# Hybrid encoder block on one core: the first expert tile's input from early rows and 0/1 products, tile tables by matmuls

## The reference, cut to what matters

```python
logits = (hf @ w_router + b_router)
top_vals, top_idx = lax.top_k(logits, 4)
gates = softmax(top_vals)
flat_e = top_idx.reshape(-1)
order = argsort(flat_e)                    # pairs sorted by expert
xs = hf[order // 4]
sizes = bincount(flat_e, length=32)
gu = ragged_dot(xs, w_gate_up, sizes) + b_gate_up[e_sorted]
gate, up = minimum(gu[:, :1024], 7), clip(gu[:, 1024:], -7, 7)
act = (up + 1) * (gate * sigmoid(1.702 * gate))
out = (ragged_dot(act, w_down, sizes) + b_down[e_sorted]) * gates_sorted
h = h + segment_sum(out, token_of)
```

## Time and profile before

| what | us |
|---|---|
| median of 3 runs | 2186.11 |
| lowest and highest | 2184.25, 2188.28 |
| profiled execution | 2184.28 |
| its span | 2182.2 |
| granted TensorE clock, mean | 0.982 |

### The profile page before, as it was taken

The page is one execution under the profiler, slowest core; times in us unless marked ns, Lnnn a source line. Parts: engine busy times, 40 slices in busy tenths (PEclk is TensorE's granted clock), DMA queues, the critical chain, the costliest instruction groups (busy, mean ns, idle before and its releaser), DMA issues.

```text
span 2182.2 us, 42210 instructions
## 1 busy us (share of the span) xinstructions
PE 2081.2 (95%) x15590; PEld 1884.4 (86%) x15591; DVE 937.7 (43%) x2300; ACT 433.0 (20%) x1072; POOL 556.5 (26%) x641
## 2 busy tenths in 40 slices
PE   7999999999976889999999999999999999999996
PEld 6777777755546889999999999999999999999996
DVE  1322332233443444554454455444455544454544
ACT  1333333232321111112111111211112111112110
POOL 2211111100223223223323222323222322223332
PEclk9999999999988999999999999999999999999998
DMA  7000000141315889999998998999899998999994
GB/s 254 28 11 11 11 11 1 36 167 49 144 50 184 253 264 324 314 287 295 276 294 280 307 299 278 304 284 312 282 312 302 307 291 262 312 314 306 319 304 113
DMA packets 240403, 477.30 MB, mean 219 GB/s; under 512 B 44607, under 2 KB 60747, under 8 KB 240304
## 3 DMA queue, kind: packets, MB, share of 16 engines
q1 hardware_dynamic: 182416, 433.09, 59.3%
...
...
## 4 chain that ended last, share of the span: by engine, by line
PE 90%; DVE 3%; issue 3%; DMA 1%; ACT 1%; POOL 0%; DVEq 0%; ACTq 0%; SPq 0%; POOLq 0%
PE psum L1011 42%; PE psum L1027 23%; PE psum L811 8%; PE psum L960 5%; PE psum L850 3%; PE psum L919 2%; PE psum L828 2%; PE psum L918 1%; PE psum L892 1%; PE psum L940 1%; PE psum L903 1%; DMA area<-in_w_in 1%; DVE area L1319 1%; DVE area L1314 1%; PE psum L990 1%
## 5 line engine op out<-in xcount | busy, mean ns | idle before, releaser
L1011 PE MATMUL psum<-area 128*128 128x128 f32 (+3 forms) x8192 | 979.0, 282 | 38.2 <-issue 20.1
L1011 PEld LDWEIGHTS psum<-area 128*128 128x128 f32 x8192 | 970.3, 192 | 43.6 <-issue 43.6
L1027 PE MATMUL psum<-area 128*128 128x128 f32 (+3 forms) x4096 | 496.3, 282 | 2.2
L1027 PEld LDWEIGHTS psum<-area 128*128 128x128 f32 x4096 | 484.5, 191 | 11.7 <-DVE area L1319 11.3
L605 POOL DMA_INDIRECT out<-area x160 | 255.9, 1600 | 68.5 <-issue 39.1
L1293 DVE STREAM_TRANSPOSE area<-area 32x320 f32<-32x320 f32 x512 | 257.1, 502 | 15.0
L1300 DVE TENSOR_SCALAR area<-psum,area 128x160 f32<-128x160 f32 x256 | 86.5, 379 | 347.0 <-PE psum L1011 347.0
L1314 DVE TENSOR_SCALAR area<-psum,area 128x160 f32<-128x160 f32 x256 | 86.5, 379 | 266.2 <-PE psum L1011 265.5
L602 POOL COPY area<-area 128x5 uint32 x32 | 6.0, 188 | 714.7 <-ACT area L779 714.7
L811 PE MATMUL psum<-area 128*128 128x128 f32 x1536 | 178.4, 277 | 9.6 <-ACT area L692 4.0
L811 PEld LDWEIGHTS psum<-area 128*128 128x128 f32 x1536 | 175.0, 193 | 14.3 <-ACT area L688 5.8
...
## 6 DMA issues: line engine op xcount, KB each, us to landing
area<-in_w_gate_up SPq DMA_DIRECT2D x256, 1024.0 KB, 6.8
area<-in_w_down SPq DMA_DIRECT2D x128, 1024.0 KB, 5.3
...
area<-in_x SPq DMA_DIRECT2D x9, 512.0 KB, 12.3
...
```

The costliest lines, as they stand in the source:

```text
L1011: ins = mm(dst, w_gu[piece][:, k, c * P:(c + 1) * P], xT[:, PART * s + k, 0:width], start=(s == 0 and k == 0 and c % 2 == 0), stop=(s == 1 ...
L1027: ins = mm(bank[4 + d // 3][:, (d % 3) * SLOTS:(d % 3) * SLOTS + width], w_dn[q][:, kk, d * P:(d + 1) * P], actT[:, 2 * q + kk, 0:width], ...
```

## The change

Tile 0 is now always a tile of expert 0 (a table value makes expert 0 use at least one tile), so that its weights needn't be chosen. Its input `xT` comes from three sources instead of one gather:

- rows of blocks 0 to 5: SyncE reads the list of expert 0 when the scatters of these blocks have landed, GpSimd gathers what it finds (`early_rows`, zeroed before; indices outside are skipped), and VectorE turns the five groups, two behind HB of block 7 and three behind the tables;
- blocks 6 and 7: `by_chunk` holds the normed rows in the order of the 128-wide chunks (block 6 copied by GpSimd, block 7 made by VectorE), `is_place` is a 0/1 matrix of tokens by slots, and 8 matmuls per block form the products in PSUM (steps XTa, XTb, XT); VectorE adds them to `xT`.

The counts come as a column by a matmul, the tiles of each expert by one compare and one sum, and both running sums by one matmul with the constant `upto`. VectorE writes the last normed block and its places only behind all that. In the loop ScalarE issues the next list behind two sigmoids, not ahead of them; GpSimd waits no more for the gathered rows, and VectorE waits for each group apart.

```diff
+    parts["levels"][0, 0] = -1.0
+    parts["floor"] = np.where(p == 0, 1.0, -1.0e6)
+    parts["upto"] = np.concatenate([p <= e[None, :], p < e[None, :]], 1).astype(np.float32)
...
+                    ("HA", e), ("XTa", e - 1), ("HB", e), ("XTb", e - 1), ("RT", e), ("RK", e), ("XT", e)]
 
 
...
-                weights(0, 0, piece, early_in)
+                weights(0, 0, piece, w_exp_in[piece])
             for i in range(NT):
                 b = i % H_ROWS
+                if i == NT - 1:
+                    sp.wait_ge(listed, 16 * (NT - DIRECT) * TOPK)
+                    for q in range(Q):
+                        sp.dma_start(early_list[32 * q:32 * q + 32, :, :],
+                                     lists[0:SLOTS, :].rearrange("(g j) c -> j g c", j=32)).then_inc(early_in, 16)
                 sp.wait_ge(h_ready, 2 * (i + 1))
                 sp.dma_start(out[0][i * P:(i + 1) * P, :], h_sb[b]).then_inc(h_out, 16)
                 sp.wait_ge(hf_ready, i + 1)
-                sp.dma_start(hf_dram[i * P:(i + 1) * P, :], hf).then_inc(hf_out, 16)
+                sp.dma_start(hf_dram[i * P:(i + 1) * P, :], hf if i < NT - 1 else hf_last).then_inc(
+                    hf_out if i < NT - DIRECT else hf_late, 16)
...
-            sp.wait_ge(early_in, 16 * PIECES)
-            with sp.If(e0 < 1):
-                for piece in range(PIECES):
-                    sp.sem_inc(w_exp_in[piece], 16)
-            with sp.Else():
-                for piece in range(PIECES):
-                    weights(e0, 0, piece, w_exp_in[piece])
-            refill(e0, 0, 1)
+            refill(0, 0, 1)
             with sp.Fori(1, MAX_TILES) as t:
                 with sp.If(t < n_tiles):
...
 
             wait(empty_in, 16)
+            wait(pv_done, NT * HEADS)
+            g.tensor_copy(quarter, K["quarter"].to_broadcast([P, G])).then_inc(pick_ready, 1)
+            g.memset(early_rows, 0.0).then_inc(early_picked, 1)
             for n in range(NT):
+                if n == NT - DIRECT:
+                    wait(hf_ready, n + 1)
+                    g.tensor_copy(by_chunk[0].rearrange("t (k p) -> t p k", k=KD), hf.rearrange("t (p k) -> t p k", k=KD)).then_inc(by_chunk_ready, 1)
+                    wait(early_in, 16 * Q)
+                    wait(pick_ready, 1)
+                    g.tensor_tensor(early_pick, early_list[:, :, 0], quarter, ALU.add).then_inc(early_picked, 1)
+                    wait(early_picked, 2)
+                    wait(hf_out, 16 * (NT - DIRECT))
...
+                    sigmoid(t * 2, 0)
+                    sigmoid(t * 2, 1)
                     act.wait_ge(list_read, t + 1)
                     load_list(t + 1)
-                    sigmoid(t * 2, 0)
-                    sigmoid(t * 2, 1)
                     flush_rows(t)
...
                         ins = mm(bank[7][:, 2 * P:2 * P + E], hfT[:, k, :], w_r[:, k, :], start=(k == 0), stop=(k == KD - 1))
                     ins.then_inc(rt_done, 1)
+                if kind in ("XTa", "XTb", "XT"):
+                    j = n - (NT - DIRECT)
+                    pe.wait_ge(placed, j + 1)
+                    pe.wait_ge(by_chunk_ready, j + 1)
+                    for d in {"XTa": range(KD // 2), "XTb": range(KD // 2, KD), "XT": range(KD)}[kind]:
+                        ins = mm(bank[4 + d // 3][:, (d % 3) * SLOTS:(d % 3 + 1) * SLOTS], by_chunk[j][:, d * P:(d + 1) * P],
+                                 is_place[:, j, :], start=(j == 0 and d % 3 == 0), stop=(j == 1), skip_group_check=True)
+                        if j and d in (2, 5, 7):
+                            ins.then_inc(first_done, 1)
+                if kind == "RK" and n == NT - 1:
+                    pe.wait_ge(mask_ready, NT)
+                    mm(bank[3][0:E, 0:1], cums[:, NT, :], ones[:, 0:1], start=True, stop=True).then_inc(count_mm, 1)
                 if kind == "RK":
-                    rank_of(n, bank[4 + n - (NT - 2)][:, 0:E]).then_inc(rank_mm, 1)
-
-            mm(bank[6][:, 0:E], ones, cums[:, NT, :], start=True, stop=True).then_inc(rank_mm, 1)
+                    rank_of(n, bank[4 if n < NT - 1 else 1][:, 0:E]).then_inc(rank_mm, 1)
+                if kind == "RK" and n == NT - 1:
+                    mm(bank[0][:, 2 * E:3 * E], ones, cums[:, NT, :], start=True, stop=True)
+                    pe.wait_ge(used_ready, 1)
+                    mm(bank[0][:, 0:2 * E], used_b[0:E, :], K["upto"][0:E, :], start=True, stop=True).then_inc(total_mm, 1)
+
 
             pe.wait_ge(tab_ready, 1)
             for c, col in enumerate((0, 3, 2)):
...
                     V.tensor_copy(hfT[:, 4:8, :], bank[3].rearrange("p (k n) -> p k n", k=4)).then_inc(hb_read, 1)
+                    if n == NT - 1:
+                        V.scalar_tensor_tensor(by_chunk[1].rearrange("t (k p) -> t p k", k=KD), h_sb[n % H_ROWS].rearrange("t (p k) -> t p k", k=KD),
+                                               rs_h[:, n:n + 1], gf_row.rearrange("t (p k) -> t p k", k=KD),
+                                               ALU.mult, ALU.mult).then_inc(by_chunk_ready, 1)
+                        early_turn(range(2))
...
-                    dve.wait_ge(rank_mm, n - (NT - 2) + 1)
-                    ch.link(V.tensor_tensor(rank_at, bank[4 + n - (NT - 2)][:, 0:E], K["room"], ALU.add))
+                    j = n - (NT - DIRECT)
+                    if j == 0:
+                        dve.wait_ge(lanes_in, 16)
+                    ch.link(V.tensor_scalar(off_list[:, j:j + 1], mask[:, n, 0:1], -OUTSIDE, OUTSIDE, ALU.mult, ALU.add))
+                if kind == "RK" and n == NT - 1:
+                    dve.wait_ge(count_mm, 1)
+                    ch.link(V.tensor_copy(count_c[0:E, :], bank[3][0:E, 0:1]))
+                    ch.link(V.tensor_scalar(over[0:E, :], K["levels"][0:E, :], count_c[0:E, 0:1], None, ALU.is_lt))
+                    ch.link(V.tensor_reduce(used_c[0:E, :], over[0:E, :], AX_X, ALU.add))
+                    V.tensor_copy(used_b[0:E, :], used_c[0:E, 0:1].to_broadcast([E, P])).then_inc(used_ready, 1)
+                if kind == "RK":
+                    dve.wait_ge(rank_mm, j + 1)
+                    ch.link(V.tensor_tensor(rank_at, bank[4 if n < NT - 1 else 1][:, 0:E], K["room"], ALU.add))
+                    V.tensor_scalar(is_place[:, j, :], lane_at, rank_at[:, 0:1], off_list[:, j:j + 1],
+                                    ALU.subtract, ALU.is_equal).then_inc(placed, 1)
+                if kind == "RK" and n < NT - 1:
                     places(n)
 
 
-            dve.wait_ge(rank_mm, 3)
-            dve.wait_ge(hf_out, 16 * NT)
-            dve.wait_ge(h_out, 16 * NT)
-            ch.link(V.tensor_copy(count, bank[6][:, 0:E]))
-            ch.link(V.tensor_scalar(used, count, 0.0, None, ALU.is_gt))
-            for j in range(1, LEVELS):
...
-            total = cum[:, src, :]
-
-
-            tile_no = K["tokp"]
-            ch.link(V.tensor_tensor(first_t, total, used, ALU.subtract))
+            dve.wait_ge(total_mm, 1)
+            tile_no, total = K["tokp"], bank[0][:, 0:E]
+            V.tensor_copy(n_i, total[:, E - 1:E])
             V.tensor_scalar(past_e, total, tile_no, None, ALU.is_le)
-            ch.link(V.tensor_scalar(at_e, first_t, tile_no, None, ALU.is_le))
+            ch.link(V.tensor_scalar(at_e, bank[0][:, E:2 * E], tile_no, None, ALU.is_le))
             V.tensor_reduce(tab[:, 0:1], past_e, AX_X, ALU.add)
-            V.tensor_tensor(prod[:, 0, :], past_e, used, ALU.mult)
             ch.link(V.tensor_tensor(at_e, at_e, past_e, ALU.subtract))
-            V.tensor_reduce(tab[:, 1:2], prod[:, 0, :], AX_X, ALU.add)
-            ch.link(V.tensor_tensor(prod[:, 1, :], at_e, count, ALU.mult))
-            ch.link(V.tensor_reduce(tab[:, 2:3], prod[:, 1, :], AX_X, ALU.add))
+            ch.link(V.tensor_tensor(prod, mid(at_e, 2), bank[0][:, E:3 * E].rearrange("p (c e) -> p c e", c=2), ALU.mult))
             V.tensor_scalar(tab[:, 0:1], tab[:, 0:1], float(E - 1), None, ALU.min)
+            ch.link(V.tensor_reduce(tab[:, 1:3], prod, AX_X, ALU.add))
             ch.link(V.tensor_scalar(tab[:, 1:2], tab[:, 1:2], tile_no, -float(SLOTS), ALU.subtract, ALU.mult))
-            V.tensor_tensor(tab[:, 2:3], tab[:, 2:3], tab[:, 1:2], ALU.subtract)
+            V.tensor_scalar(tab[:, 2:3], tab[:, 2:3], tab[:, 1:2], K["floor"], ALU.subtract, ALU.max)
             ch.link(V.scalar_tensor_tensor(tab[:, 3:4], tab[:, 0:1], float(ROOM), tab[:, 1:2], ALU.mult, ALU.add))
             V.tensor_scalar(tab[:, 3:4], tab[:, 3:4], float(LISTED - SLOTS), None, ALU.min).then_inc(tab_ready, 1)
-            V.tensor_copy(n_i, total[:, E - 1:E])
+            early_turn(range(2, G))
 
             dve.wait_ge(tab_turned, 1)
             turned = bank[2][0:1, 0:3 * P].rearrange("p (c n) -> p c n", c=3)
             V.tensor_copy(tabs_i[0:1, :, :], turned[:, :, 0:TABLE]).then_inc(tables_ready, 1)
+            dve.wait_ge(early_turned, G)
+            for b in range(3):
+                m = min(3, KD - 3 * b)
```

(6 more changed lines are left out.)

74 lines of the change are left out of this document (45 added, 29 removed).

## The result

The changed kernel takes 2295.7 us, the kernel before 2185.2 beside it on the same chip: a ratio of 1.050, 95% interval 1.049 to 1.052. The forecast was 2174.3. The profiled execution has a span of 2293.2 us, against 2182.2 for the profiled one of before.

The account below looks back on a forecast made before the run. The prediction took the serial chain from last mask to tile 0's first down product as the bound. That product 12.6 us earlier, less 0.8 for the clock, gave 11.8 off 2186.11: 2174.3 us, range 2168.5 to 2181.5.

Parts of the forecast that it names:

- rival 4: Expert loop: added code shifts every body, more 5.8 us fetch openings; two cancel the gain, three give 2191.7 us; chance 0.05.
- The main sum: Front part and tile 0: down product 12.6 us earlier, less 0.8 for the clock, gains 11.8 us, giving 2174.3; chance 0.62.
- strided product on VectorE: Ahead of the router's result: the product in chunk order, written with a stride, takes 2.1 us, 1.28 as the other end.
- last mask: End of the router's part: the last mask is ready at 645.15 instead of 644.45, 0.7 us late.
- 8 matmuls of block 7: TensorE between mask and tables: 3.6 us, from 2.2 at 2.4 GHz and 4.4 at 1.2 GHz, the clock rising inside them.
- m: The moment when the last mask is ready, forecast at 645.15; later steps are counted from it.
- clock charge: Tile 0: the stall before the down product may lower the clock, costing 1.6 us or nothing; half, 0.8, was charged.
- rival 3: Ahead of the router's result: early rows come late and VectorE waits, gain 6 to 9 us, 2177 to 2180; chance 0.13.
- The mask to the tables: From the last mask to the tables: 7.5 us instead of 10.3, the matmuls of block 7 ending last, not the table operations.
- The new wait of VectorE's register load: Between xT and the first expert matmul: TensorE waits 3.1 us for gate_read, raised behind VectorE's queued work.
- The sigmoid's chain: Tile 0: ScalarE's sigmoid, behind the list and outT's zeroing, stalls TensorE about 2.2 us; down product at 675.65.
- No change in the loop from the list's new place: Expert loop: issuing the next list behind two sigmoids costs nothing, with 15 us of slack.

Follow-up runs that it names:

- e10: The changed kernel with its loop moved by 181 instructions, 176 of them increments in a branch never taken, to its place in the kernel before: 2178.0 us, ratio 0.9961.
- e9: The changed kernel with three extra fp32 matmuls behind the last router products, keeping TensorE busy up to the mask: 2271.9 us, ratio 1.040.
- e11: The changed kernel with three extra matmuls, places of block 7 and bank freeing moved earlier, and 164 increments in a branch never taken: 2174.3 us, ratio 0.9953.
- e17: Like e11, with GpSimd's zeroing of the output area also put ahead of its wait for the first list: 2168.1 us, ratio 0.9908.
- e3: The changed kernel with ScalarE issuing the next list ahead of its two sigmoids again, TensorE's program untouched: 2303.9 us, ratio 1.053.
- 83: TensorE's loop starts 83 instructions later than in the kernel before: the changed kernel with 8 semaphore increments ahead of TensorE's first wait, 2271.8 us.
- 87: TensorE's loop starts 87 instructions later than in the kernel before: e8 and e9, 2271.6 and 2271.9 us.
- 75: TensorE's loop starts 75 instructions later than in the kernel before: the changed kernel 2295.7 us, the kernel before with 75 increments 2313.5, e3 2303.9.
- e8: Like e9, with two VectorE moves: places of block 7 ahead of the wait for turned tables, banks freed right behind xT: 2271.6 us, ratio 1.038.

## Why the prediction was wrong, by its own steps

**The step that failed is rival 4**, in chance and in price. Its mechanism was named: the added code shifts every loop body, and a jump to code that isn't there stalls. I gave it 0.05, on the ground that 15 openings took only 20.1 us in the kernel before, and priced it at one to three more openings of 5.8 us. Both came from one wrong step: the old trace was read as a sample of what openings cost, when it shows one regime. In it the loop stays loaded, and two jumps cost two packets each. In the other every change of width can find its blocks thrown out, and the price is 92 us of openings (25 waits instead of 15) and 27 us of longer expert matmuls behind them. The profile's page held what would have told them apart: 36 instruction packets, every block about once, and a loop of over six. That such a loop can stand in seven or eight blocks, and that 75 instructions decide it, was open to counting, and by this account the chance of a bad place was near 57 in 256, about 0.22, with a price of about 118 us. Even so the likeliest time would have stayed near 2174; the low chance of "slower" and the upper end were wrong.

**The main sum, against e10.** At the place of before, the change takes 2178.0 us, 3.7 more than the forecast and inside its range; the gain at tile 1 is 3.2 us short of the sum. Two terms account for that: the down product starts 9.9 us earlier instead of 12.6 (688.20 less 678.27), and the clock took 1.6 us instead of 0.8. Its TensorE began the last transposes within 0.2 us of the kernel before, so its rows can be held against the forecast.

| step | forecast | e10 |
|---|---|---|
| strided product on VectorE | 2.1 | 1.99 |
| last mask | 645.15 | 644.80 |
| 8 matmuls of block 7 | 3.6, end m + 5.7 | 4.50, end m + 6.8 |
| tables (cast ends) | m + 7.5 | m + 7.9 |
| xT | m + 9.1 | m + 9.5 |
| first expert matmul | 657.45 | 657.88 |
| places of block 7 start | 655.55 | 655.38 |
| GpSimd has the list of tile 0 | 667.8 to 668.8 | 670.68 |
| first down product | 675.65 | 678.27 |
| clock charge | 0.8 | 1.6 |
| gain at tile 1 | 11.8 | 8.6 |

VectorE's and GpSimd's rows in e10, columns as before:

```profile
639.39 1.99 DVE L1262 SCALAR_TENSOR_TENSOR area<-area,attn_stat 128x1024 f32<-128x1024 f32 x1
641.23 1.13 DVE L1153 STREAM_TRANSPOSE area<-area 128x256 f32<-128x256 f32 x2
...
644.61 0.19 DVE L1293 TENSOR_TENSOR area<-area 128x32 f32<-128x32 f32 x1
...
652.37 0.36 DVE L1339 CAST area<-psum 1x204 int32<-1x204 f32 x1 [1.40 <-PE psum L1058]
652.66 1.59 DVE L1344 TENSOR_TENSOR area<-area,psum 128x480 f32<-128x480 f32 x3
...
655.38 0.72 DVE L1158 SCALAR_TENSOR_TENSOR area<-consts,area 128x32 f32<-128x32 f32 x4
```

- **Ahead of the mask: right.** No early turn waited for its rows (rival 3 is out), and the strided write took 1.99 us for the same 1024 elements that took 1.28.
- **The mask to the tables: right in shape, a term too small.** The matmuls of block 7 ended behind the table operations, as said, but the clock did not rise inside them. At the lower level (granted clock 0.52 from 647.1 to 651.5 us in e10) they took the 4.4 us that I had as the other end. e9 and e11 confirm the cause, 2.44 us at the upper level (1.00 in both).
- **The new wait of VectorE's register load: right.** From xT to the first expert matmul were 3.6 us (654.25 to 657.88), against a forecast 3.1. The 5.5 us of the profile count from TensorE's own last work. It was worth removing (e11).
- **The sigmoid's chain: mechanism right, 2.6 us too short.** The last scatter was issued at 661.25, against a forecast 661.45; the list was the late piece. From the first issue of its load to GpSimd's first use were 3.6 us in the kernel before (656.22 to 659.80; the 4.3 us of the forecast begin with the register load at 655.53, which no longer stands in the way). In e10 they were 6.6:

```profile
664.08 2.28 ACTq L808 DMA_DIRECT2D area<-token_lists  x4
...
673.47 1.28 ACT L812 ACT_TABLE_LOAD   x1 [30.13 <-issue]
```

```profile
670.68 0.19 POOL L627 TENSOR_TENSOR area<-area 128x5 uint32<-128x5 uint32 x1 [8.46 <-DMA area<-token_lists]
```

```profile
663.49 11.09 SPq L470 DMA_DIRECT2D area<-in_w_gate_up  x4
```

The earlier start of TensorE also lets SyncE send the next weights, 4 MB, 0.6 us ahead of the list. I had carried the old duration over from idle DMA engines (6 and 11% busy from 655 to 658 and from 658 to 660 us before) to a stretch where they are full (66% from 664 to 666 us in e10, 96% and more from there to 672). The loads in e10 land 4.1 to 4.9 us after their issue. In e11 the first load goes out 0.5 us ahead of the weights (661.63 against 662.18) and lands in 1.9 us, the three behind it take 2.4 to 5.0. That fits the weights as the cause; no run held them back. e17 shows that the list held the down product only through the zeroing behind it: with the zeroing moved ahead, the product doesn't wait, though GpSimd first uses the list at 672.74.
- **The clock charge: half of what came.** The 64 down matmuls behind the stall took 9.04 us, against 7.41 in the earlier trace rows.
- **No change in the loop from the list's new place: right**, by e3 and e10.

**What stays open.** Why 83 and 87 cost 24 us less than 75, why the packets at one shift range from 85 to 99 between e9 and e8 (the profiled execution of e8 was 17 us above its median, so the refetching may differ from one execution to the next), and why whole widths go by without a refetch and another jump takes eight blocks. Whether the outer or the inner loop's length sets the stretch can't be told from its bounds.
